# Last scaling of three of eight output tiles split between ScalarE and GpSimd, with the stores in another order

## The chip, the cores and the metric

The kernel runs on one core of a Trainium2 chip. The metric is the device time of one execution in microseconds. One core has five engines that run side by side, each with its own queue of instructions, and they meet at semaphores: TensorE (PE in the profile), VectorE (DVE), ScalarE (ACT), GpSimd (POOL) and SyncE (SP), the last of which issues only transfers here. The kernel is written by hand: the order of the instructions in each queue is the order of the code.

## The reference

One transformer layer on 1024 tokens of width 1024: four token mixers (top-k sparse attention, an mLSTM, banded attention, differential attention), a gated sum of them, then a mixture of 32 experts of which each token takes two, and a last RMS norm. The change concerns only what stands after the experts, which in the reference is this:

```python
def rmsnorm(x, g, eps=1e-6):
    xf = x.astype(jnp.float32)
    y = xf * lax.rsqrt(jnp.mean(xf * xf, axis=-1, keepdims=True) + eps)
    return (y * g.astype(jnp.float32)).astype(x.dtype)

# hier_moe: the experts' rows, weighted, are added up by token
out = jnp.zeros((t, d), h.dtype).at[row_tok].add((ys * row_w[:, None]).astype(h.dtype))
# hybrid_layer
return x + hier_moe(h2, ...)
# reference
return rmsnorm(x, final_norm_g)
```

## The kernel before, in words

The program runs through `project`, `attend`, `mix`, `route`, `experts` and `combine`. `combine` is the last 43 us of 1849. It works on eight tiles of 128 tokens (partitions) by 1024 columns, each 512 KB in fp32. The residual stream `s.x2[t]` lies in SBUF throughout, and the experts' rows lie in HBM in `ys`.

- **GpSimd** issues two indirect gathers for each tile (L2531): `ya[t]` and `yb[t]`, the two expert rows of each token, 16 transfers in all, in the order of the tiles.
- **VectorE** waits for both (`y_in[t]`), adds them into `x2[t]` with their gates (L2562, L2564: two `scalar_tensor_tensor`, each with two tensors in SBUF as inputs, and each followed by a wait for its own completion, the helper `link`), tells ScalarE (`summed`, L2566), and then finishes the tile before, `finish(t - 1)`: a reciprocal of 128 numbers (L2555), and the last scaling `ya = x2 * rms * fg` (L2556), a third `scalar_tensor_tensor` with two tensors in SBUF. `fg` holds the weights of the last norm on all partitions. After the last tile it does `finish(7)`.
- **ScalarE** squares and sums each row (L2542) and takes the root (L2545), into `rms`.
- **SyncE** waits for the scaled tiles and stores them in the order of the tiles (L2521), and then waits until all eight stores have landed (L2523).

Each engine's queue is in order. So a wait in SyncE's queue holds back all stores behind it, and the scaling of tile t - 1 stands between the sums of tile t and of tile t + 1 on VectorE.

Of other places the prediction uses rows from GpSimd's and VectorE's work earlier in the program: copies of a bias table (L390 to L392), a product of two tensors in SBUF (L400), the norm's scaling at the program's start (L597), and in the experts' loop a copy of 96 indices (L2247) beside VectorE's subtractions (L2452).

Of the kernel before, what the change touches and what calls it, by code (L numbers as in the profile page):

```python
# [20 lines left out]
ALU = mybir.AluOpType  # L21
ACT = mybir.ActivationFunctionType
# [5 lines left out]
NT = SEQ // P  # L28
# [44 lines left out]
def chained(eng, chain):  # L73


    sem, count = chain

    def link(ins):
        count[0] += 1
        ins.then_inc(sem, 1)  # L80
        eng.wait_ge(sem, count[0])
    return link


def build(nc, a):

    ctx = ExitStack()
    with ctx:
# [140 lines left out]
        s.sem = late_sem  # L229
        experts(nc, a, s)  # L230
        combine(nc, a, s)
    return nc

# [2268 lines left out]
def combine(nc, a, s):  # L2502

    sb, sem = s.sb, s.sem
    ya = [sb(f"ya{i}", [P, DM], 96 + 4 * i) for i in range(NT)]
    yb = [sb(f"yb{i}", [P, DM], 128 + 4 * i) for i in range(NT)]
    fg = sb("fg", [P, DM], 160)
    junk = sb("junk6", [P, DM], 164)
    ssq, rms, eps = sb("ssq6", [P, NT], 200), sb("rms6", [P, NT], 200.0625), sb("eps6", [P, 1], 200.125)
    fg_in, eps_set = sem("fg_in"), sem("eps_set")  # L2510
    squared = s.squared
    y_in = [sem(f"y_in{t}") for t in range(NT)]
    stored = s.x_in
    summed, rooted, final = sem("summed6"), sem("rooted6"), sem("final")
    with nc.Block() as block:
        @block.sync
        def _(sp):
            sp.dma_start(fg[:, :], a["g_final"].partition_broadcast(P)).then_inc(fg_in, 16)
            for t in range(NT):
                sp.wait_ge(final, t + 1)  # L2520
                sp.dma_start(a["out"][t * P:(t + 1) * P, :], ya[t][:, :]).then_inc(stored[t], 16)  # L2521
            for t in range(NT):
                sp.wait_ge(stored[t], 48)  # L2523

        @block.gpsimd
        def _(pool):
            pool.memset(eps[:, :], EPS).then_inc(eps_set, 1)  # L2527
            for t in range(NT):
                for k, dst in enumerate((ya, yb)):
                    col = k * NT + t  # L2530
                    pool.indirect_dma_start(dst[t][:, :], None, s.ys,  # L2531
                                            bass.IndirectOffsetOnAxis(ap=s.row_of[:, col:col + 1].bitcast(U32), axis=0)
                                            ).then_inc(y_in[t], 16)

        @block.scalar
        def _(act):
            act.wait_ge(eps_set, 1)
            for t in range(NT):
                act.wait_ge(summed, t + 1)
                if t:  # L2540
                    act.wait_ge(rooted, t)
                nc.scalar.activation(junk[:, :], s.x2[t][:, :], ACT.Square,  # L2542
                                     accum_out=ssq[:, t:t + 1]).then_inc(squared, 1)
                act.wait_ge(squared, NT + t + 1)
                nc.scalar.activation(rms[:, t:t + 1], ssq[:, t:t + 1], ACT.Sqrt, bias=eps[:, 0:1],  # L2545
                                     scale=1.0 / DM).then_inc(rooted, 1)

        @block.vector
        def _(dve):
            link = chained(dve, s.dve_chain)  # L2550
            dve.wait_ge(fg_in, 16)

            def finish(t):
                dve.wait_ge(rooted, t + 1)
                link(nc.vector.reciprocal(rms[:, t:t + 1], rms[:, t:t + 1]))  # L2555
                nc.vector.scalar_tensor_tensor(out=ya[t][:, :], in0=s.x2[t][:, :], scalar=rms[:, t:t + 1], in1=fg[:, :],  # L2556
                                               op0=ALU.mult, op1=ALU.mult).then_inc(final, 1)

            for t in range(NT):
                x2 = s.x2[t][:, :]  # L2560
                dve.wait_ge(y_in[t], 32)
                link(nc.vector.scalar_tensor_tensor(out=x2, in0=ya[t][:, :], scalar=s.gates[:, 0, t:t + 1], in1=x2,  # L2562
                                                    op0=ALU.mult, op1=ALU.add))
                link(nc.vector.scalar_tensor_tensor(out=x2, in0=yb[t][:, :], scalar=s.gates[:, 1, t:t + 1], in1=x2,  # L2564
                                                    op0=ALU.mult, op1=ALU.add))
                nc.vector.engine_nop().then_inc(summed, 1)  # L2566
                if t:
                    finish(t - 1)
            finish(NT - 1)
# [56 lines left out]
```

## Time and profile before

| | us |
|---|---|
| median of 3 runs | 1848.51 |
| lowest and highest | 1845.42, 1849.59 |
| the profiled execution, its own time | 1850.85 |
| span of its records | 1849.1 |
| `combine`, from its first gather to the end of the span | 42.8 |
| VectorE busy from 1806 to 1849.1 | 31.6 |
| ScalarE busy there | 12.8 |
| GpSimd busy there | 16.7 |

The span goes from the first to the last record of the profiled execution; 1.75 us of its own time lie outside the span. Over the whole program TensorE is busy 94% of the span, but in `combine` it has no work at all. Times in the rows are microseconds from the span's start.

### The profile page before, as it was taken

The page shows a single profiled execution, that of the slowest core. Times are in us where ns is not written, and L with a number is a line of the kernel's source. Part 1 is how long each engine was busy: PE and PEld are TensorE (multiplying, and loading weights), DVE is VectorE, ACT ScalarE, POOL GpSimd, SP SyncE. Part 2 cuts the span into 40 slices and gives each one's busy share as a digit, 9 for nine tenths or more (in the row PEclk, how much of TensorE's full clock was granted, in tenths as well). Part 3 has the DMA queues.
Part 4 walks back from the last instruction along what each step waited for, and adds up shares of the span by engine and source line. Part 5 has one row for each costly group of instructions (what it writes and reads, how often), then busy time and mean ns, then how long its engine had stood idle before and what let it go on. Part 6 is the DMA issues. An engine that isn't in the chain of part 4 may idle for free. (4 is left out here: it accounts for less than half of the span.)

```text
span 1849.1 us, 24075 instructions
## 1 busy us (share of the span) xinstructions
PE 1737.8 (94%) x8726; PEld 1318.3 (71%) x8726; DVE 1456.1 (79%) x2108; ACT 941.6 (51%) x1207; POOL 151.2 (8%) x129
## 2 busy tenths in 40 slices
PE   7999999999999999999999989959999999999990
PEld 7768877777777777777777767747777777777760
DVE  5587869989788878766528975679999999999976
ACT  6533121133344445554656520137788778777862
POOL 1100000000000000000000000002121221221103
PEclk9999999999999999999999989969999999999995
DMA  5202222112343421412316830199999999999947
GB/s 199 69 6 87 74 86 69 58 57 75 128 157 114 128 63 58 148 52 77 107 35 221 309 127 35 47 374 343 395 403 396 396 405 395 401 399 394 404 180 288
DMA packets 75920, 358.76 MB, mean 194 GB/s; under 512 B 8636, under 2 KB 11228, under 8 KB 49340
## 3 DMA queue, kind: packets, MB, share of 16 engines
q1 hardware_dynamic: 66364, 324.08, 46.9%
q0 software_dynamic: 5888, 20.97, 3.5%
q10 hardware_dynamic: 3584, 12.58, 1.7%
q8 instruction: 52, 0.85, 0.2%
q14 instruction: 32, 0.26, 0.0%
HBM read 301.63 MB, written 55.98 MB: 193 GB/s over the span
## 5 line engine op out<-in xcount | busy, mean ns | idle before, releaser
L2444 DVE TENSOR_TENSOR wa_lo<-wa,w_hi 128x2048 fp32r<-128x2048 f32 x127 | 287.6, 2286 | 15.5 <-ACT w_hi L2349 14.1
L2349 ACT ACTIVATE w_hi<-wa 128x2048 fp32r<-128x2048 f32 x127 | 242.8, 1915 | 63.0 <-PE psum L2293 36.4
L1470 PE MATMUL psum<-h_hi,w_hi 128*128 128x512 f32 x512 | 213.3, 417 | 4.0 <-DVE w_lo L153 2.1
L1470 PE MATMUL psum<-h_hi,w_lo 128*128 128x512 f32 x512 | 205.9, 402 | 0.0
L1470 PE MATMUL psum<-h_lo,w_hi 128*128 128x512 f32 x512 | 203.5, 397 | 0.0
L167 DVE MAX8 top<-sel 128x8 f32<-128x384 f32 (+5 forms) x192 | 171.3, 892 | 4.8
L165 DVE MATCH_REPLACE8 sel<-top,sel 128x384 f32<-128x384 f32 (+5 forms) x192 | 168.1, 876 | 0.0
L2273 PE MATMUL psum<-w_hi,xT_hi 128*96 128x512 f32 x512 | 164.9, 403 | 1.9 <-DVE xT_lo L2460 1.9
L2452 DVE TENSOR_TENSOR wb_lo<-wd,w_hi 128x2048 fp32r<-128x2048 f32 x62 | 139.4, 2289 | 33.4 <-ACT w_hi L2359 33.4
L2273 PE MATMUL psum<-wa_lo,xT_hi 128*96 128x512 f32 x512 | 160.7, 395 | 0.0
L2273 PE MATMUL psum<-w_hi,xT_lo 128*96 128x512 f32 x512 | 160.7, 395 | 0.0
L1470 PEld LDWEIGHTS psum<-h_hi,w_hi 128*128 128x128 f32 x512 | 97.0, 190 | 46.5 <-issue 18.9
L1197 ACT ACTIVATE pt<-psum 128x512 f32<-128x512 f32 (+3 forms) x144 | 61.2, 471 | 119.3 <-PE psum L1490 119.1
L2359 ACT ACTIVATE w_hi<-wd 128x2048 fp32r<-128x2048 f32 x62 | 118.7, 1915 | 3.8 <-PE psum L2273 2.4
L922 PE MATMUL psum<-h_hi,w_hi 128*128 128x512 f32 x288 | 117.6, 408 | 0.0
L1470 PEld LDWEIGHTS psum<-h_hi,w_lo 128*128 128x128 f32 x512 | 96.9, 189 | 25.3 <-issue 5.1
L922 PE MATMUL psum<-h_hi,w_lo 128*128 128x512 f32 x288 | 112.7, 391 | 0.0
L922 PE MATMUL psum<-h_lo,w_hi 128*128 128x512 f32 x288 | 112.4, 390 | 0.0
L1470 PEld LDWEIGHTS psum<-h_lo,w_hi 128*128 128x128 f32 x512 | 97.2, 190 | 19.6 <-issue 2.7
L2273 PEld LDWEIGHTS psum<-wa_lo,xT_hi 128*96 128x96 f32 x512 | 83.4, 163 | 36.0
L2273 PEld LDWEIGHTS psum<-w_hi,xT_lo 128*96 128x96 f32 x512 | 83.3, 163 | 35.8 <-issue 0.2
L2273 PEld LDWEIGHTS psum<-w_hi,xT_hi 128*96 128x96 f32 x512 | 78.6, 164 | 29.5 <-DVE xT_lo L2460 2.2
(388 smaller groups left out, 3396.5 us busy)
## 6 DMA issues: line engine op xcount, KB each, us to landing
wa<-expert_up SPq DMA_DIRECT2D x128, 1024.0 KB, 11.2
wd<-expert_down SPq DMA_DIRECT2D x64, 1024.0 KB, 11.3
w<-w_gate SPq DMA_DIRECT2D x32, 512.0 KB, 4.2
gate_pre<-gate_out SPq DMA_DIRECT2D x64, 256.0 KB, 2.6
gate<-gate_pre SPq DMA_DIRECT2D x32, 512.0 KB, 6.1
ys<-yo ACTq DMA_DIRECT2D x32, 384.0 KB, 6.9
w<-w_T SPq DMA_DIRECT2D x18, 512.0 KB, 3.8
ys<-zeros SPq DMA_DIRECT2D x7, 1152.0 KB, 5.9
```

Of the source, the lines that this page charges most:

```text
L165: link(nc.vector.match_replace(sc, top8[:, :], sc, TAKEN))
L167: link(nc.vector.max(top8[:, :], sc))
L922: ins = nc.tensor.matmul(psum[:, bank + h, :], w[:, k, :], x[:, k, h * 512:(h + 1) * 512], start=(k == 0 and r == 0), stop=(k == KC - 1 an ...
L1197: nc.scalar.activation(dst, src, ACT.Copy).then_inc(pt_copied, 1)
L1470: ins = nc.tensor.matmul(psum[:, 7, :], w[:, k, :], x[:, k, half * 512:(half + 1) * 512], start=(n == 0), stop=(n == BURST - 1))
L2273: ins = nc.tensor.matmul(psum[0:CAP, UP + m, :], x[:, k, :], w[:, c, m, :], start=(k == 0 and x is xT_hi[j] and w is not wa_lo[j][q]), sto ...
L2349: nc.scalar.activation(hi_a(j, q).rearrange("p c m n -> p (c m n)"), wa[j][q][:, :, :, :].rearrange("p c m n -> p (c m n)"), ACT.Copy).the ...
L2359: nc.scalar.activation(dst.rearrange("p f n -> p (f n)"), wb[j][q][:, :, :].rearrange("p f n -> p (f n)"), ACT.Copy).then_inc(b_high, 1)
L2444: nc.vector.tensor_tensor(wa_lo[j][q][:, :, :, :].rearrange("p c m n -> p (c m n)"), wa[j][q][:, :, :, :].rearrange("p c m n -> p (c m n)" ...
L2452: nc.vector.tensor_tensor(wb_lo[j][q][:, :, :].rearrange("p f n -> p (f n)"), wb[j][q][:, :, :].rearrange("p f n -> p (f n)"), high.rearra ...
```

## The change

Tiles 1, 3 and 5 (the second, fourth and sixth) are no longer scaled by VectorE. VectorE still takes the reciprocal for them. ScalarE then multiplies `x2[t]` by the row factor into `ya[t]`, behind its root of tile t + 1, and GpSimd multiplies `ya[t]` by `fg` in place, behind all 16 gathers. SyncE stores the tiles in the order 0, 2, 1, 4, 3, 6, 5, 7, and waits for GpSimd's semaphore before tiles 1, 3 and 5. Nothing else in the program changes, and there are no further table loads on ScalarE.

```diff
+    ON_POOL = (1, 3, 5)
+    own = [t for t in range(NT) if t not in ON_POOL]
@@ sync
-            for t in range(NT):
-                sp.wait_ge(final, t + 1)
+            for t in (0, 2, 1, 4, 3, 6, 5, 7):
+                if t in ON_POOL:
+                    sp.wait_ge(final_pool, ON_POOL.index(t) + 1)
+                else:
+                    sp.wait_ge(final, own.index(t) + 1)
                 sp.dma_start(a["out"][t * P:(t + 1) * P, :], ya[t][:, :]).then_inc(stored[t], 16)
@@ gpsimd, behind the gathers
+            pool.wait_ge(fg_in, 16)
+            for n, t in enumerate(ON_POOL):
+                pool.wait_ge(scaled, n + 1)
+                pool.tensor_tensor(ya[t][:, :], ya[t][:, :], fg[:, :], ALU.mult).then_inc(final_pool, 1)
@@ scalar, behind the root of tile t
+                if t - 1 in ON_POOL:
+                    act.wait_ge(inverted, ON_POOL.index(t - 1) + 1)
+                    nc.scalar.activation(ya[t - 1][:, :], s.x2[t - 1][:, :], ACT.Copy,
+                                         scale=rms[:, t - 1:t]).then_inc(scaled, 1)
@@ vector, finish(t)
                 dve.wait_ge(rooted, t + 1)
+                if t in ON_POOL:
+                    nc.vector.reciprocal(rms[:, t:t + 1], rms[:, t:t + 1]).then_inc(inverted, 1)
+                    return
```

VectorE's queue from the sum of tile 6 to the end, of the kernel before. In the names `x_6` is `s.x2[6]`, `ya_13441` is `ya[5]`, `ya_13442` is `ya[6]`, `ya_13443` is `ya[7]`, and ISA is the empty instruction that tells ScalarE of the sum:

```order
L2562 SCALAR_TENSOR_TENSOR x_6_9459<-ya_13442,gates,x_6_9459 128x1024
L2564 SCALAR_TENSOR_TENSOR x_6_9459<-yb_13450,gates,x_6_9459 128x1024
L2566 ISA
L2555 RECIPROCAL rms_13455<-rms_13455 128x1
L2556 SCALAR_TENSOR_TENSOR ya_13441<-x_5_9458,rms_13455,fg 128x1024
L2562 SCALAR_TENSOR_TENSOR x_7_9460<-ya_13443,gates,x_7_9460 128x1024
L2564 SCALAR_TENSOR_TENSOR x_7_9460<-yb_13451,gates,x_7_9460 128x1024
L2566 ISA
L2555 RECIPROCAL rms_13455<-rms_13455 128x1
L2556 SCALAR_TENSOR_TENSOR ya_13442<-x_6_9459,rms_13455,fg 128x1024
L2555 RECIPROCAL rms_13455<-rms_13455 128x1
L2556 SCALAR_TENSOR_TENSOR ya_13443<-x_7_9460,rms_13455,fg 128x1024
```

The same stretch of VectorE's queue in the changed kernel:

```order
L2579 SCALAR_TENSOR_TENSOR x_6_9459<-ya_13442,gates,x_6_9459 128x1024
L2581 SCALAR_TENSOR_TENSOR x_6_9459<-yb_13450,gates,x_6_9459 128x1024
L2583 ISA
L2570 RECIPROCAL rms_13455<-rms_13455 128x1
L2579 SCALAR_TENSOR_TENSOR x_7_9460<-ya_13443,gates,x_7_9460 128x1024
L2581 SCALAR_TENSOR_TENSOR x_7_9460<-yb_13451,gates,x_7_9460 128x1024
L2583 ISA
L2572 RECIPROCAL rms_13455<-rms_13455 128x1
L2573 SCALAR_TENSOR_TENSOR ya_13442<-x_6_9459,rms_13455,fg 128x1024
L2572 RECIPROCAL rms_13455<-rms_13455 128x1
L2573 SCALAR_TENSOR_TENSOR ya_13443<-x_7_9460,rms_13455,fg 128x1024
```

The scaling of tile 5 between the two sums is gone, its reciprocal stays; the same holds for tiles 1 and 3 further up.

The end of GpSimd's queue in the changed kernel, where before it ended with the two gathers (`ya_13437` and `ya_13439` are `ya[1]` and `ya[3]`):

```order
L2537 DMA ya_13442<-ys,row_of 128x1024
L2537 DMA yb_13450<-ys,row_of 128x1024
L2537 DMA ya_13443<-ys,row_of 128x1024
L2537 DMA yb_13451<-ys,row_of 128x1024
L2543 TENSOR_TENSOR ya_13437<-ya_13437,fg 128x1024
L2543 TENSOR_TENSOR ya_13439<-ya_13439,fg 128x1024
L2543 TENSOR_TENSOR ya_13441<-ya_13441,fg 128x1024
```

Three products of two tensors in SBUF have come in behind the last gather.

## Rows read from the trace of the kernel before

**Rows 1.** Chain that ended last, in order of time, from 1838.91: start, length, what.

```profile
1838.91 0.15 DVE rms L2555
...
1839.09 1.28 DVE ya L2556
1840.37 1.21 DVE x L2562
...
1841.61 1.30 DVE x L2564
...
1842.98 1.16 ACT junk L2542 x2
...
1844.16 0.30 ACT rms L2545
...
1844.69 1.29 DVE ya L2556
```

**Rows 2.** Groups from 1805 to 1850: busy us, mean ns, idle before and releaser.

```profile
L2556 DVE SCALAR_TENSOR_TENSOR ya<-x,rms,fg 128x1024 f32<-128x1024 f32 x8 | 10.3, 1285 | 0.3
L2562 DVE SCALAR_TENSOR_TENSOR x<-ya,gates,x 128x1024 f32<-128x1024 f32 x8 | 10.3, 1282 | 19.6 <-DMA yb<-ys,row_of 19.6
...
L2542 ACT ACTIVATE junk<-x 128x1024 f32<-128x1024 f32 x8 | 8.5, 1057 | 30.1 <-DVEq L2566 30.1
...
L2545 ACT ACTIVATE rms<-ssq,eps 128x1 f32<-128x1 f32 x8 | 2.4, 294 | 0.2
L2542 ACT ACTIVATION_READ_ACCUMULATOR junk<-x 128x1 f32 x8 | 1.5, 186 | 0.0
...
L2555 DVE RECIPROCAL rms<-rms 128x1 f32<-128x1 f32 x8 | 1.3, 159 | 0.4
```

**Rows 3.** Issue of yb for tiles 3 and 7, then the landing of each after its issue.

```profile
1816.09 0.94 POOL L2531 DMA_INDIRECT yb<-ys,row_of  x1 [0.30 <-issue]
1826.58 0.97 POOL L2531 DMA_INDIRECT yb<-ys,row_of  x1 [0.30 <-issue]
```
```profile
yb<-ys,row_of POOLq DMA_INDIRECT x1, 6.2
```
```profile
yb<-ys,row_of POOLq DMA_INDIRECT x1, 9.5
```

**Rows 4.** Timeline, start and length, of VectorE and GpSimd work that overlaps or stands alone.

```profile
19.26 1.29 DVE L597 SCALAR_TENSOR_TENSOR xs<-xs,rstd,gain 128x1024 f32<-128x1024 f32 x1
19.37 2.92 POOL L390 COPY far<-rel 128x2044 f32<-128x2044 f32 x1 [16.53 <-DMA rel<-rel]
22.25 0.82 POOL L391 COPY far<-rel 128x768 f32<-128x768 f32 x1
23.01 0.41 POOL L392 COPY far<-rel 128x260 f32<-128x260 f32 x1
```
```profile
1228.96 0.18 POOL L2247 COPY idx<-tok_of 96x1 int32 x1 [13.40 <-PE psum L2153]
```
```profile
1272.20 4.49 DVE L2452 TENSOR_TENSOR wb_lo<-wd,w_hi 128x2048 fp32r<-128x2048 f32 x2 [0.98 <-ACT w_hi L2359]
1273.12 1.41 POOL L2247 COPY idx<-tok_of 96x1 int32 x1 [13.30 <-PE psum L2153]
```

**Rows 5.** GpSimd's product of two SBUF tensors, line L400: ns min/median/max, first and last start.

```profile
L400 POOL TENSOR_TENSOR oB<-oB,gainB x8: 725/732/737, 52.4 to 57.2; 128x256 f32<-128x256 f32 x8
```

**Rows 6.** VectorE's first sum, line L2562: ns min/median/max.

```profile
L2562 DVE SCALAR_TENSOR_TENSOR x<-ya,gates,x x8: 1278/1279/1301, 1812.4 to 1840.3; 128x1024 f32<-128x1024 f32 x8
```

**Rows 7.** The last two stores: issue; landing; then windows of the transfer (last columns: clock, DMA share, GB/s).

```profile
1844.44 0.33 SPq L2521 DMA_DIRECT2D out<-ya  x1
```
```profile
1846.00 0.33 SPq L2521 DMA_DIRECT2D out<-ya  x1
```
```profile
out<-ya SPq DMA_DIRECT2D x1, 512.0 KB, 2.6
```
```profile
1846.50:1847.00 0.50, 0.00 (x0) 0.00 (x0) 0.00 (x0) 0.00 (x0) 0.00 (x0) 0.50 0.42 164
1847.00:1847.50 0.50, 0.00 (x0) 0.00 (x0) 0.00 (x0) 0.00 (x0) 0.00 (x0) 0.50 1.04 426
1847.50:1848.00 0.50, 0.00 (x0) 0.00 (x0) 0.00 (x0) 0.00 (x0) 0.00 (x0) 0.50 1.00 410
1848.00:1848.50 0.50, 0.00 (x0) 0.00 (x0) 0.00 (x0) 0.00 (x0) 0.00 (x0) 0.50 0.20 74
```

More of the change, by code:

```diff
@@ L2514, in combine @@
     summed, rooted, final = sem("summed6"), sem("rooted6"), sem("final")
+    inverted, scaled, final_pool = sem("inverted6"), sem("scaled6"), sem("final_pool")
+    ON_POOL = (1, 3, 5)
+    own = [t for t in range(NT) if t not in ON_POOL]
     with nc.Block() as block:
```

## Prediction

> **What bounds the kernel now.** The change lies wholly in the last 43 us, so I read first the chain of work that ended last, in order of time, and only its end. In [rows 1] the reader is to see that VectorE carries it almost alone: reciprocal, scaling of the tile before, two sums, again and again; a round is 4.04 us, six rounds in a row from tile 1 to tile 7. Only at the very end does ScalarE come in (1.16 + 0.30 us, square and root of tile 7), then the last reciprocal and scaling, which ends at 1844.69 + 1.29 = 1845.98. From there to the end of the span are 3.1 us of store. The groups of the same stretch [rows 2] say the same: the 24 large operations of VectorE take 1.28 us each and have no idle time before them but 19.6 us for gathers, all of it before tiles 0 and 1. ScalarE waits 30.1 us for VectorE. So an instruction taken from VectorE between tile 1 and tile 7 shortens the path, if nothing else holds it. Next I ask what would be late after that: gathers, ScalarE, GpSimd, the stores.
>
> **Part 1, three scalings leave VectorE: -3.7 us.** Each is 1.285 us [rows 2]. In [rows 1] the time from the end of a reciprocal (1839.06) to the start of the following sum, which overlaps the end of the scaling by 0.08, is about 1.3; without the scaling the sum starts about 0.05 after or at the reciprocal's end. That is 1.24 us a piece, and 3 x 1.24 = 3.7.
>
> **Part 2, the gathers stay hidden.** A faster VectorE asks for them earlier. The sum of tile 3 would start at about 1822.9; its last gather is issued at 1816.09 and lands 6.2 later, at 1822.3 [rows 3]. The tightest later one is tile 7: 1826.58 + 9.5 = 1836.1 [rows 3], against a sum that would start at 1840.37 - 3.7 = 1836.6 if VectorE gained everything. Cost 0; if that cover were gone by a store's more traffic it would be some tenths, but the changed order puts a store less among the gathers.
>
> **Part 3, ScalarE: off the path, 0.** After the root of tile 2, 4, 6 it has one more pass over 1024 columns. The nearest row is its square, 1.06 us [rows 2]. A round of ScalarE is 1.06 + 0.19 + 0.29 = 1.54 and becomes 2.7 in three rounds, where VectorE gives it at least the 2.6 of two sums. What is queued behind the new wait for the reciprocal is the square of the next tile; the reciprocal is ready by then, 0.2 us after the sum, while ScalarE is busy 1.6 with square and root. Before the last tile the copy of tile 5 ends 2.75 us after tile 6's sum, just before tile 7's sum ends at 2.83, so the last square isn't late.
>
> **Part 4, GpSimd's three products and what they do to VectorE: this decides.** Their own price first. The trace has a product of two SBUF tensors on GpSimd at 256 columns: 0.73 us each, eight started from 52.4 to 57.2, so one each 0.70 [rows 5]. What of it is fixed, the copies tell: 0.41 us for 260 columns, 0.82 for 768 [rows 4], so about 0.2 fixed in a recorded duration and 0.14 in the distance of starts (22.25 to 23.01 is 0.76 for 768). So at 1024 columns 4 x 0.56 + 0.14 = 2.4 us; the bound above is 4 x 0.73 = 2.9, the one below the rate of a copy, 1.0. I take 2.4, since it is the same operation and only its length differs.
>
> Now the two engines beside each other. In [rows 4] GpSimd's copy of 2044 columns is recorded from 19.37, while VectorE works on two SBUF inputs from 19.26 to 20.55, and takes 2.92. By the copies beside it it needs 0.14 + 2044 x 0.81 ns = 1.8; 20.55 + 1.74 is just where it ends, 22.29. It stood still for the whole of VectorE's instruction and then ran at its own speed. In the experts' loop a copy of 96 indices takes 0.18 us alone and 1.41 beside a VectorE pair of 2 x 2.25 us, and ends at 1274.53, the moment in which VectorE's first operation ends, though the second is queued right behind it (28 such copies have a median of 1.47). So GpSimd waits out the VectorE instruction that runs, and gets in at its end, ahead of or beside the next one. What happens to a VectorE instruction with two SBUF inputs that finds GpSimd in a long operation, this trace doesn't show: the long ones of GpSimd met no such VectorE work. The nearest row is one sum that lasted 1.301 instead of 1.278 [rows 6], beside a gather's issue that reads only its indices. So VectorE's loss per product lies between 0 and the whole 2.4 us. I take the whole, since in the direction that the trace shows the waiting side got no share until the other had ended.
>
> The Trainium skill, "SBUF — State Buffer", section "Who interferes with whom", says the same of both directions: a VectorE instruction with two SBUF inputs and a GpSimd instruction that reads SBUF take turns on a shared read interface, and whichever starts first keeps it for its whole length. The first direction this trace bears out (1.41 us in place of 0.18), the second no row here shows. The "GPSIMD Engine Reference", section 3.1, gives 4497 ns for such a product of 2048 columns; half, 2.25 us, would make the sum below 0.4 us smaller, an estimate from that page.
>
> Place by place: the first product stands behind the 16th gather, whose issue ends at about 1827.8. VectorE is then in the first sum of tile 4, to 1828.2. The product gets in there and holds back the second sum: 2.35 us. The second product (tile 3) is ready 2.75 us after the sum of tile 4, just when the sum of tile 5 ends; VectorE still has its reciprocal and semaphores (0.2), then the scaling of tile 4 waits: 2.4 - 0.2 = 2.2. The third (tile 5) comes in the same way at the end of tile 7's sum and holds back the scaling of tile 6: 2.2. Should VectorE come first at one of these points, the product only moves behind that instruction and holds the next; the sum stays. Together +6.75, less 0.15 for each start of a product in which it doesn't read yet, +6.3.
>
> **Part 5, the stores: +0.9 us.** The last store takes 0.8 us from issue to its first data and 1.25 us of data (512 KB at 410 to 426 GB/s, see the windows), landing in 2.6 [rows 7]. In the forecast case tiles 6 and 5 are both ready when the scaling of tile 6 ends, E. SyncE issues 6 at E and 5 at E + 0.33 (its issue takes 0.33), and tile 7 is scaled at E + 1.57, as 1844.44 to 1846.00 [rows 7]. Three transfers of 1.25 follow each other from E + 0.8: data ends at E + 4.55, against E + 1.57 + 0.8 + 1.25 = E + 3.6 for tile 7 alone. If the third product comes behind tile 6's scaling, stores 6 and 5 are apart and this term is 0.
>
> **Sum.** -3.7 + 6.3 + 0.9 = +3.5 us. On the profiled execution: 1850.85 + 3.5 = 1854.35, its span 1849.1 to 1852.6. That execution lies 2.3 above the median of the runs, so for the median: 1848.5 + 3.5 = 1852.0. With the product at 2.9 it is 1.5 more, 1853.5; without the term of the stores 1851.1; with both small (hold 2.1) 1850.5.
>
> **Rivals.**
>
> *VectorE isn't held (chance 0.14).* If a product that runs leaves VectorE's instructions their full speed, the 3.7 are gained in full, and the last product ends before tile 7's scaling: the copy of tile 5 is done 0.1 before tile 7's sum ends, + 2.4, against + 3.1 for VectorE's end. 1848.5 - 3.7 = 1844.8, faster. For it speaks only that no row shows VectorE held; against it, that the other direction is a full stop.
>
> *Sharing, or GpSimd comes last (0.16).* The two take turns in pieces, so that VectorE loses about half of each product: -3.7 + 3 x 1.2 = -0.1. Or VectorE always goes first when it has work, so that the third product waits until VectorE's last instruction has ended, at 1845.98 - 3.7 = 1842.3. It ends at 1844.7, and SyncE's queue has tile 7 behind tile 5: data of both ends at 1844.7 + 0.8 + 2.5 = 1848.0, where before it ended at 1848.1. That too is 0: 1848.4, no change. For it: a price between the ends; against it, the index copy that got in between two VectorE instructions.
>
> *The hold is longer than I make it (part of the first case, slower).* If a product at 1024 columns takes 2.9, by four times the 256 column row, VectorE loses 3 x 2.7 and the sum is +5. It decides from a hold of 2.2 us each on: above it the change passes 0.2% with the stores' term.
>
> The Trainium skill, "Perfetto Trace Analysis", section "Optimizing Scalar/DVE Operations", warns that work handed from VectorE to GpSimd may not help, since they share an SBUF port; the sum above is what that would mean here.
>
> **How the numbers follow.** The forecast case has 0.70: VectorE stands still for each product. Within it the time lies between 1850.5 and 1853.5 by the bounds, with a run's own scatter of some 2 us (1845.42 to 1849.59 before). The bound of 0.2%, 3.7 us, about what a measurement of this kernel can tell from no change, cuts through it at 1852.2: 0.39 above, 0.31 within. From the first rival (1844.8, just at the lower bound) 0.10 is faster and 0.04 within; from the second 0.13 within, 0.02 faster, 0.01 slower. So faster 0.12, same 0.48, slower 0.40. The time is that of the likeliest case, 1852.0. The range leaves out most of the first rival and the upper end with scatter: 1845.5 to 1855.0; the forecast case's own range is 1849.5 to 1855.
>
> **What the changed profile would show.** VectorE's operations at L2579, L2581 or L2573 with a maximum of 3 to 3.6 us in place of 1.3, three of them, each with a GpSimd product before it: right. All 21 at 1.28 and VectorE's last one ending near 1842.3: the first rival. Products of 4 us and more: GpSimd waits instead. The copy on ScalarE near 1.06, no wait of VectorE for gathers from tile 2 on, and stores of tiles 6 and 5 issued 0.33 apart. A product of 1.5 or of 4 us alone, or gathers that land later, would make the forecast wrong.

## The result

| | us |
|---|---|
| before, median of 20 runs (lowest, highest) | 1850.08 (1845.42, 1852.94) |
| changed, median of 20 runs (lowest, highest) | 1853.61 (1850.57, 1856.74) |
| ratio, with 95% interval | 1.0019 (1.0012 to 1.0026) |
| profiled execution of the changed kernel, its own time and span | 1856.19, 1854.4 |

The changed kernel is slower by 0.19%, 3.5 us between the medians; the interval, 2.2 to 4.8 us, excludes zero and straddles the 0.2% line. That is the sum of the prediction in size (+3.5) and its likeliest case. The time itself, forecast as 1852.0, came out 1.6 higher, since the forecast stood on the 1848.51 of three runs of the kernel before, and twenty give 1850.08. What follows asks whether the terms are as right as their sum.

The two spans differ by 5.3, but 2.4 of it lies ahead of `combine` (its first gather is issued at 1808.72, before at 1806.31), where the change touches nothing. So the traces are compared from that issue on. "VectorE's end" below is the time from the issue of the first gather to the end of VectorE's last operation, the "tail" is the time from there to the end of the span, and the "stretch" their sum:

| | VectorE's end | tail | stretch |
|---|---|---|---|
| before | 39.67 | 3.12 | 42.79 |
| changed | 41.39 | 4.29 | 45.68 |

Each such number is from one execution. VectorE's scaling of tile 0, ahead of which no edit takes anything from its queue or adds to it, starts 12.25 to 13.13 us after the first gather's issue in the fourteen traces. So VectorE's end can differ by up to 0.9 us between two executions before a product or a scaling left out has played any part. The lengths of single operations and the tails don't have this scatter.

The chain that ended last, of the changed kernel, in order of time (start, length, what), against [rows 1]:

```profile
1829.50 1.21 DVE x L2579
1830.70 0.02 issue
1830.73 3.25 DVE x L2581
1833.98 0.03 issue
1834.01 0.01 DVEq L2583
1834.03 0.14 DVE rms L2570
1834.17 1.20 DVE x L2579
...
1836.91 3.17 DVE ya L2573
...
1845.53 3.18 DVE ya L2573
...
1848.82 1.29 DVE ya L2573
```

VectorE still carries the chain. Behind the reciprocal of tile 3 (1834.03) the next sum starts at once: the scaling is gone. But three operations take 3.2 us, though they have the 1024 columns of those that take 1.28 in [rows 2]. The timeline of VectorE and GpSimd shows beside what they stand:

```profile
1830.32 2.57 POOL L2543 TENSOR_TENSOR ya<-ya,fg 128x1024 f32<-128x1024 f32 x1
1830.73 3.24 DVE L2581 SCALAR_TENSOR_TENSOR x<-yb,gates,x 128x1024 f32<-128x1024 f32 x1
...
1836.66 2.34 POOL L2543 TENSOR_TENSOR ya<-ya,fg 128x1024 f32<-128x1024 f32 x1 [3.77 <-ACT ya L2559]
1836.72 0.16 DVE L2572 RECIPROCAL rms<-rms 128x1 f32<-128x1 f32 x1
...
1836.91 3.17 DVE L2573 SCALAR_TENSOR_TENSOR ya<-x,rms,fg 128x1024 f32<-128x1024 f32 x1
...
1840.00 1.27 DVE L2579 SCALAR_TENSOR_TENSOR x<-ya,gates,x 128x1024 f32<-128x1024 f32 x1
...
1845.28 2.35 POOL L2543 TENSOR_TENSOR ya<-ya,fg 128x1024 f32<-128x1024 f32 x1 [6.28 <-ACT ya L2559]
1845.34 0.16 DVE L2572 RECIPROCAL rms<-rms 128x1 f32<-128x1 f32 x1
...
1845.53 3.18 DVE L2573 SCALAR_TENSOR_TENSOR ya<-x,rms,fg 128x1024 f32<-128x1024 f32 x1
```

Each long operation starts beside a product of GpSimd. The second product ends at 1839.00, the scaling beside it at 1840.08, as if it did nothing until 0.2 us before the product's end and then took its own 1.28. The two don't share in pieces either: the second and third product keep 2.34 and 2.35, as long as where they hold nobody (2.35 and 2.36 in kernels below). Nor is it that both want the same tile: the sum at 1830.73 reads `yb`, the gates and `x2`, the product beside it `ya[1]` and `fg`. What each lost is its length less 1.285: 1.96, 1.89 and 1.89, together 5.74 us. The reciprocal at 1836.72, one column with one input, ran its 0.16 within the same product.

The tail grew by 1.2 us. The windows of the last transfers (last columns: clock, DMA share, GB/s), against those of [rows 7], where the last store has the transfers to itself from 1846.50 on:

```profile
1850.00:1850.50 0.50, 0.00 (x0) 0.00 (x0) 0.10 (x1) 0.00 (x0) 0.00 (x0) 0.50 1.02 401
1850.50:1851.00 0.50, 0.00 (x0) 0.00 (x0) 0.00 (x0) 0.00 (x0) 0.00 (x0) 0.50 0.99 402
...
1852.00:1852.50 0.50, 0.00 (x0) 0.00 (x0) 0.00 (x0) 0.00 (x0) 0.00 (x0) 0.50 1.11 442
1852.50:1853.00 0.50, 0.00 (x0) 0.00 (x0) 0.00 (x0) 0.00 (x0) 0.00 (x0) 0.50 0.99 410
```

The transfers begin at about 1849.5, during VectorE's last operation, and run without a pause to about 1853.4: the last store stands behind two others.

### The profile page after: what moved, and what is told of

The parts are those of the page before. It is cut to its first block and busy times, and to the rows that moved or that the text cites. A ratio compares the mean times of both kernels' runs of the same rounds, so it can differ in the third digit from the quotient of the medians.

```text
span 1854.4 us, 24079 instructions
## 1 busy us (share of the span) xinstructions
PE 1738.8 (94%) x8726; PEld 1318.0 (71%) x8726; DVE 1459.6 (79%) x2105; ACT 945.1 (51%) x1210; POOL 158.8 (9%) x132
```

## The experiments

The theory: while GpSimd's product reads SBUF, a VectorE operation with two inputs in SBUF stands still, and the tail is the order of the stores. The rivals: ScalarE's extra passes or the traffic slow VectorE; any work of GpSimd slows it; any VectorE operation is slowed. All numbers are from traces unless they are called a ratio or a median; ratios are timed against the kernel before on the same chip, with their 95% interval. A microsecond in them is 0.05%, so the traces tell more. The diffs are against the changed kernel if not said otherwise.

### The products left out

```diff
-                pool.tensor_tensor(ya[t][:, :], ya[t][:, :], fg[:, :], ALU.mult).then_inc(final_pool, 1)
+                pool.engine_nop().then_inc(final_pool, 1)
```

> The changed kernel without GpSimd's three products (tiles 1, 3 and 5 are stored without the weights of the last norm); the semaphores, ScalarE's passes and the order of the stores stay. Measure: from the issue of the first gather to the end of the span, 42.8 us before and 45.7 changed. Theory (VectorE stands still while a product runs): the three long VectorE operations are 1.28 again, VectorE's last one ends 3.9 us earlier than before, the stores of tiles 5 and 6 are no longer together, and the stretch is about 39.0, so 3.8 below the kernel before and 6.7 below the changed one; ratio to before 0.998. Rival (ScalarE's passes or the order of the stores cost the time): VectorE's operations stay long or the last store stays late, and the stretch is 42 to 45.

Measured: VectorE's end 36.62, tail 4.16, stretch 40.78; ratio 0.9989 (0.9980 to 0.9998). Groups of the stretch (busy us, mean ns, idle before and releaser):

```profile
L2581 DVE SCALAR_TENSOR_TENSOR x<-yb,gates,x 128x1024 f32<-128x1024 f32 x8 | 10.3, 1285 | 0.3
...
L2573 DVE SCALAR_TENSOR_TENSOR ya<-x,rms,fg 128x1024 f32<-128x1024 f32 x5 | 6.4, 1285 | 0.2
L2559 ACT ACTIVATE ya<-x,rms 128x1024 f32<-128x1024 f32 x3 | 3.4, 1132 | 0.0
```

All of VectorE's operations are at 1.28 again with ScalarE's passes in place, so the long ones belong to the products. Two of my numbers missed. VectorE's end came 3.05 earlier than before, not 3.9. The missing 0.85 is time for gathers: the sum of tile 1 starts 10.18 us after the first gather's issue, before 9.73, and a wait of 0.41 us for tile 7 is new:

```profile
1836.14 1.28 DVE L2579 SCALAR_TENSOR_TENSOR x<-ya,gates,x 128x1024 f32<-128x1024 f32 x1 [0.41 <-DMA yb<-ys,row_of]
```

And the tail is 4.16 without any product, so it isn't the products that lengthen it.

### GpSimd writes and doesn't read

```diff
-                pool.tensor_tensor(ya[t][:, :], ya[t][:, :], fg[:, :], ALU.mult).then_inc(final_pool, 1)
+                pool.memset(spare[n][:, :], 1.0).then_inc(final_pool, 1)     # 2560 columns, own tile each
```

> In place of each product GpSimd fills a spare tile of 2560 columns, which reads nothing and takes about 2.3 us, as long as the product (tiles 1, 3 and 5 lack the weights). Theory (it is the second input of VectorE that is held, by GpSimd's reading): no VectorE operation is longer than 1.3, the stretch is about 39.9, since the last fill still delays the stores of tiles 5 and 7 by up to 0.9. Rival (any long GpSimd operation on SBUF holds VectorE): three VectorE operations of 3.2 us and the stretch 45 to 45.7 as in the changed kernel.

Measured: VectorE's end 35.98, tail 4.20, stretch 40.18; ratio 0.9986 (0.9977 to 0.9995).

```profile
1839.28 2.23 POOL L2544 MEMSET spare<- 128x2560 f32 x1 [4.51 <-ACT ya L2560]
...
1839.57 1.28 DVE L2574 SCALAR_TENSOR_TENSOR ya<-x,rms,fg 128x1024 f32<-128x1024 f32 x1
```

A GpSimd operation of 2.23 us lies over a whole VectorE scaling, which takes 1.28. Writing alone holds nothing; it needs GpSimd to read. The stretch was 0.3 above the 39.9 expected, within the scatter.

### The products alone, on the kernel before

```diff
+            pool.wait_ge(fg_in, 16)
+            for n, t in enumerate((1, 3, 5)):
+                pool.wait_ge(rooted, t + 2)
+                pool.tensor_tensor(spare[n][:, :], fg[:, :], fg[:, :], ALU.mult)
```

> The kernel before with three GpSimd products of the same size added behind the gathers, into spare tiles, each released by the root of tiles 2, 4 and 6; VectorE keeps all its scalings and the stores their order. Theory: each product holds one VectorE sum by about 1.95 us, together 5.9: the stretch 42.8 + 5.9 = 48.7, ratio to before 1.003; no term of the stores, since the last three tiles are apart. Rival (the loss in the changed kernel comes from ScalarE's part or from the stores): the stretch stays near 42.8 to 43.5.

Measured: VectorE's end 45.53, tail 3.13, stretch 48.66, 5.87 above before as expected; ratio 1.0022 (1.0013 to 1.0031), a little less than that. The hit is partly luck. Timeline:

```profile
1826.24 3.60 DVE L2561 SCALAR_TENSOR_TENSOR ya<-x,rms,fg 128x1024 f32<-128x1024 f32 x1
1826.84 1.91 POOL L2538 TENSOR_TENSOR spare<-fg 128x1024 f32<-128x1024 f32 x1
...
1833.99 2.83 POOL L2538 TENSOR_TENSOR spare<-fg 128x1024 f32<-128x1024 f32 x1 [5.25 <-ACT rms L2550]
...
1835.11 2.80 DVE L2569 SCALAR_TENSOR_TENSOR x<-yb,gates,x 128x1024 f32<-128x1024 f32 x1
```

The holds are 2.32, 1.51 and 1.51, together 5.3; the other half microsecond lies ahead of them (the first scaling starts 13.1 after the first gather, before 12.6), where no product has run yet. The second and third product come 0.2 us after the start of a sum; the second waits it out to 1835.07 and ends at 1836.82, 1.75 us later. In the changed kernel the first product also waits out a sum, to 1830.69 (1829.41 + 1.28), and ends 2.20 us later, at 1832.89. So a product of `fg` by itself is the shorter one, and the hold is shorter with it. Both directions are in these rows: GpSimd waits for the running sum, and the next sum waits for GpSimd.

### Half a product

```diff
-                pool.tensor_tensor(ya[t][:, :], ya[t][:, :], fg[:, :], ALU.mult).then_inc(final_pool, 1)
+                pool.tensor_tensor(ya[t][:, 0:512], ya[t][:, 0:512], fg[:, 0:512], ALU.mult).then_inc(final_pool, 1)
```

> The changed kernel, GpSimd multiplies only the first 512 of the 1024 columns (the other half of tiles 1, 3 and 5 lacks the weights). Measured so far: 0.73 us at 256 columns and 2.35 at 1024, so 1.27 at 512, and a hold of 1.96, 1.89 and 1.89 us at 1024. Theory (the hold lasts as long as the product does): each hold gets shorter by the product's 1.08, to 0.8 to 0.9 us, the three long VectorE operations take 2.1 to 2.2, VectorE's end 38.1 after the first gather's issue and the stretch 42.3 with the tail of 4.2. Rival (a hold is a fixed price of switching): they stay at 3.2 us and the stretch at 45.7.

Measured: VectorE's end 38.20, tail 4.36, stretch 42.56; ratio 1.0002 (0.9991 to 1.0012).

```profile
1832.66 1.27 POOL L2543 TENSOR_TENSOR ya<-ya,fg 128x512 f32<-128x512 f32 x1 [3.76 <-ACT ya L2559]
...
1832.92 2.10 DVE L2573 SCALAR_TENSOR_TENSOR ya<-x,rms,fg 128x1024 f32<-128x1024 f32 x1
```

The three long operations take 2.17, 2.10 and 2.08, holds of 0.89, 0.82 and 0.80. The second and third product, shorter by 1.08, hold for 1.07 and 1.10 less: a hold is the product's recorded length less 0.46 at either length, and no fixed price. (The first product's record, 1.49 here and 2.57 in the changed kernel, begins with some 0.2 us of waiting for the sum before it, so its hold is its record less 0.6.)

### The weights in PSUM for VectorE

```diff
+            nc.scalar.activation(fg_psum, fg[:, :], ACT.Copy).then_inc(fg_up, 1)
@@ vector, finish(t)
-  ... in0=s.x2[t][:, :], scalar=rms[:, t:t + 1], in1=fg[:, :],
+  ... in0=s.x2[t][:, :], scalar=rms[:, t:t + 1], in1=fg_psum,
```

> The changed kernel, but VectorE takes the weights for its scaling from a copy in PSUM, so that its scaling has one input in SBUF only. Theory (only an operation with two SBUF inputs is held): the first product holds the second sum of tile 4 as before (3.2 us); the second and third no longer hold the scalings of tiles 4 and 6, which take about 1.3; the second product then holds the first sum of tile 6 for the rest, 2.3 - 1.5 = 0.9, and the third nothing. So 3.8 of held time become 0.9 and VectorE ends 2.9 earlier; the stretch is 43 to 43.5, with the collision of the last stores. Rival (GpSimd and VectorE slow each other whatever VectorE reads): scalings of 3.2 us remain, the stretch stays at 45.7.

Measured: VectorE's end 39.75, tail 4.16, stretch 43.91; ratio 1.0006 (0.9997 to 1.0015). The third product and the scaling beside it:

```profile
1840.13 2.36 POOL L2545 TENSOR_TENSOR ya<-ya,fg 128x1024 f32<-128x1024 f32 x1 [7.80 <-ACT ya L2563]
...
1840.40 1.28 DVE L2577 SCALAR_TENSOR_TENSOR ya<-x,rms,psum 128x1024 f32<-128x1024 f32 x1
```

This is the row to set against the 3.18 at 1845.53 of the changed kernel: the same operation at the same place beside the same product, with one of its inputs in PSUM, and nothing is lost. All five scalings take 1.28. VectorE's gain fell short of 2.9 (it was 1.6) and the stretch is 0.4 above what I allowed, since the first two products came at other places than I had worked out and met two sums, which still read twice from SBUF:

```profile
1826.96 3.18 DVE L2583 SCALAR_TENSOR_TENSOR x<-ya,gates,x 128x1024 f32<-128x1024 f32 x1
...
1830.18 3.24 DVE L2585 SCALAR_TENSOR_TENSOR x<-yb,gates,x 128x1024 f32<-128x1024 f32 x1
```

### The stores of tiles 5 and 6 exchanged

```diff
-            for t in (0, 2, 1, 4, 3, 6, 5, 7):
+            for t in (0, 2, 1, 4, 3, 5, 6, 7):
```

> The changed kernel with the stores of tiles 5 and 6 exchanged (0, 2, 1, 4, 3, 5, 6, 7), nothing else. From the first gather's issue the changed kernel has 41.4 us to VectorE's end and 4.3 from there to the end of the span; before had 39.7 and 3.1. Theory (the longer tail comes from the order: tile 5 is ready 1.1 us before tile 6 and waits behind it in SyncE's queue, so that three transfers of 1.25 us stand in a row): VectorE's end stays at 41.4, the tail falls to 3.1 to 3.4, the stretch from 45.7 to 44.7. Rival (the tail is longer since the last transfers are slower or later for another reason): tail 4.2.

Measured: VectorE's end 41.45, tail 3.22, stretch 44.67; ratio 1.0003 (0.9994 to 1.0012). One microsecond of the loss was the order alone: tile 5 is ready when its product ends (1847.63 in the changed kernel) and waits in SyncE's queue behind tile 6 (1848.71), so that three transfers of 1.25 us meet at the end.

### First sums in PSUM too

```diff
@@ on top of the weights in PSUM: the first sum goes to PSUM, the second reads it there
-  scalar_tensor_tensor(out=x2, in0=ya[t][:, :], scalar=s.gates[:, 0, t:t + 1], in1=x2,
+  scalar_tensor_tensor(out=part, in0=ya[t][:, :], scalar=s.gates[:, 0, t:t + 1], in1=x2,
-  scalar_tensor_tensor(out=x2, in0=yb[t][:, :], scalar=s.gates[:, 1, t:t + 1], in1=x2,
+  scalar_tensor_tensor(out=x2, in0=yb[t][:, :], scalar=s.gates[:, 1, t:t + 1], in1=part,
```

> As the kernel with the weights in PSUM, and VectorE also writes the first sum of each tile to PSUM, so that the second sum has one input in SBUF; only the first sum of each tile still has two. Theory: long VectorE operations are to be found at the first sum only (L number of the sum of ya), one or two of them, held together 1.5 to 2.8 us where the changed kernel has 5.7; second sums and scalings all 1.28 to 1.35. VectorE's end 37 to 38.5 after the first gather's issue, tail 4.2 (the order 6, 5, 7 stays), stretch 41.5 to 42.7. Rival (VectorE is slowed by reading or writing PSUM): operations of 1.4 and more, and the stretch above 43.

Measured: VectorE's end 39.34, tail 4.19, stretch 43.53; ratio 1.0001 (0.9992 to 1.0010).

```profile
1823.15 4.02 DVE L2584 SCALAR_TENSOR_TENSOR psum<-ya,gates,x 128x1024 f32<-128x1024 f32 x1
...
1823.72 2.35 POOL L2546 TENSOR_TENSOR ya<-ya,fg 128x1024 f32<-128x1024 f32 x1
...
1832.62 1.99 DVE L2584 SCALAR_TENSOR_TENSOR psum<-ya,gates,x 128x1024 f32<-128x1024 f32 x1
```

The place was right, only first sums are held, and PSUM costs nothing (second sums and scalings 1.281 us), so the rival's sign is absent, although its stretch, above 43, came. The size was not right: I had allowed 1.5 to 2.8 of holds and it is 3.4, since the first product holds for 2.7 and not 1.9. That sum started 0.57 us before the product's recorded start and yet stood still from about its own start on. The product follows directly on the last gather's issue there, and GpSimd seems to have begun to read before its record starts. The last section returns to this.

### x2 of tiles 5 and 6 in PSUM

```diff
+            for t in (5, 6):
+                nc.scalar.activation(x_psum(t), s.x2[t][:, :], ACT.Copy).then_inc(fg_up, 1)
@@ and their first sums read it there
+  in1=x_psum(t) if t in (5, 6) else x2
```

> As the one before, and ScalarE copies x2 of tiles 5 and 6 to PSUM at the start, so that their first sums have one input in SBUF too. Theory: no VectorE operation is held at all if the three products fall on tiles 5 to 7; the first product may still meet the first sum of tile 4 or 7. VectorE's end 36.5 to 37 after the first gather's issue as without products (36.6), where now the gathers' landing bounds it, tail 4.2: stretch 40.8 to 41.2, 1.8 below the kernel before (0.999). Rival (sharing is not only by SBUF inputs): some operations stay at 3.2 and the stretch above 42.

Measured: VectorE's end 38.66, tail 4.13, stretch 42.79, the same as before; ratio 1.0003 (0.9994 to 1.0013). One hold is left, the first sum of tile 4 with 4.02 again, a hold of 2.7, more than the 1.6 to 2 us by which the stretch missed. The second and third product hold nothing.

### The first product later

```diff
@@ on top of that: the first product also waits for the root of tile 4
+                if n == 0:
+                    pool.wait_ge(rooted, 5)
```

> As the kernel with x2 of tiles 5 and 6 in PSUM (stretch 42.8, one operation of 4.02 us), but GpSimd's first product also waits for the root of tile 4, so that it isn't directly behind the last gather and meets only VectorE work with one SBUF input. Theory (the 4.02 is the first sum of tile 4, which still has two SBUF inputs and is held by that product, from half a microsecond before its recorded start): no VectorE operation above 1.3, VectorE's end 38.7 - 2.7 = 36.0, up to 36.6 with waits for gathers, the stretch 40.2 to 40.9. Rival (the 4.02 is the price of something else in PSUM or of the gathers): it stays, the stretch stays at 42.8.

Measured: VectorE's end 35.56, tail 4.18, stretch 39.74; ratio 0.9988 (0.9977 to 0.9998). No VectorE operation is above 1.3 us, and the stretch is 0.5 below the range, within the scatter. A wait added to GpSimd's queue made the stretch 3 us shorter.

### Tiles 1, 2 and 3 instead, with and without PSUM

```diff
-    ON_POOL = (1, 3, 5)
+    ON_POOL = (1, 2, 3)
-            for t in (0, 2, 1, 4, 3, 6, 5, 7):
+            for t in range(NT):
```

On the changed kernel, all in SBUF:

> The changed kernel with tiles 1, 2 and 3 handed over and the stores in the order of the tiles, all inputs in SBUF as in the kernels before and changed. Theory (in the fastest kernel so far, stretch 39.9, it is the inputs in PSUM that avoid the holds, not the choice of tiles): three holds, together 5.5 to 6.5 us, against 3.9 taken from VectorE; its end 41.3 to 42.3, the tail 3.1, the stretch 44.4 to 45.4, ratio about 1.001. Rival (the choice of tiles does it): no or one hold, the stretch 40 to 41.5.

Measured: VectorE's end 41.81, tail 3.14, stretch 44.95; ratio 1.0011 (1.0002 to 1.0020). Three holds of 1.7, 2.0 and 1.8, together 5.4, so the choice of tiles doesn't avoid them. The three products, one behind the other, are stretched in their turn:

```profile
1826.48 9.26 POOL L2543 TENSOR_TENSOR ya<-ya,fg 128x1024 f32<-128x1024 f32 x3
...
1827.30 2.96 DVE L2579 SCALAR_TENSOR_TENSOR x<-ya,gates,x 128x1024 f32<-128x1024 f32 x1
1830.30 3.24 DVE L2581 SCALAR_TENSOR_TENSOR x<-yb,gates,x 128x1024 f32<-128x1024 f32 x1
...
1833.78 3.06 DVE L2573 SCALAR_TENSOR_TENSOR ya<-x,rms,fg 128x1024 f32<-128x1024 f32 x1
```

The single products start at 1826.48, 1829.14 and 1832.42 and take 2.69, 3.31 and 3.33: the engines take strict turns here, product, sum, product, sum, product, scaling.

On top of weights, first sums and x2 of tiles 5 and 6 in PSUM:

> As the one before, but tiles 1, 2 and 3 are the ones handed over and the stores go in the order of the tiles, so that the last tiles are scaled by VectorE. Theory: the products lie between the end of the gathers' issue (21.5 us after the first) and 30, VectorE's end is 36.5 to 37, the tail 3.1 to 3.3 as before: stretch 39.8, 3 us below the kernel before, ratio 0.998. Rival (the gathers or the stores in the middle become the bound): VectorE waits 1 us and more for tiles 5 to 7, and the stretch is 41 to 42.

Measured: VectorE's end 36.81, tail 3.08, stretch 39.89; ratio 0.9983 (0.9972 to 0.9994). The same kernel in another set of runs:

> The same kernel as e10_tiles_1_2_3 once more: weights, first sums and x2 of tiles 5 and 6 in PSUM, tiles 1, 2 and 3 handed over. Expected as there: stretch 39.9 against 42.8 before, ratio 0.998 to 0.9985. If the first run owed its 0.9983 to scatter, the ratio is 0.9995 or above.

Measured: VectorE's end 36.88, tail 3.09, stretch 39.97; ratio 0.9980 (0.9971 to 0.9989), median 1845.62. Its products and VectorE's operations beside them:

```profile
1826.02 6.99 POOL L2551 TENSOR_TENSOR ya<-ya,fg 128x1024 f32<-128x1024 f32 x3
...
1826.96 1.29 DVE L2591 SCALAR_TENSOR_TENSOR psum<-ya,gates,psum 128x1024 f32<-128x1024 f32 x1 [0.25 <-DMA yb<-ys,row_of]
1828.29 1.28 DVE L2594 SCALAR_TENSOR_TENSOR x<-yb,gates,psum 128x1024 f32<-128x1024 f32 x1
...
1829.80 1.28 DVE L2585 SCALAR_TENSOR_TENSOR ya<-x,rms,psum 128x1024 f32<-128x1024 f32 x1
```

Without holds the stretch is 2.9 and 2.8 us below the kernel before, and both ratios are below 1, so this kernel is faster than before by 0.2%, and than the changed kernel (1.0019) by about 0.4%. What is missing to the forecast 3.7 went to gathers: VectorE waits three times 0.25 to 0.34 us for them after tile 0 in this trace, for tiles 1, 4 and 5, and the sum of tile 1 starts 0.5 us later than before.

## Why the prediction was right

**Part 1, the scalings leave VectorE.** Forecast -3.7. From the start of a reciprocal to the start of the next sum it is 1.39 us with the scaling (1838.90 to 1840.29 in the timeline of the kernel before) and 0.08 without (1825.31 to 1825.39 in the changed kernel), 1.31 each, 3.9 in all. I had let the sum start at the reciprocal's end or after it; it starts 0.08 before it.

**Part 2, the gathers.** In the changed kernel VectorE waits for none after tile 1, as forecast. But the cover was as thin as it looked: in the kernel without products VectorE waits 0.41 us for tile 7, whose last gather lands 10.3 us after its issue there, against 9.5 before, 9.8 in the changed kernel and 8.8 in the one that only writes. Why it varies isn't shown. The first rival, too, was mis-sized. The kernel without products stands for it, and gained 2.0 us, not 3.7: 0.65 less on VectorE, and 1.04 of longer tail, which that rival put at nothing. It would have given some 1846.5 in place of 1844.8.

**Part 3, ScalarE.** Its new pass takes 1.13 us, not 1.06. A long round takes 2.52 (1825.36 to 1827.88); the prediction's 2.7 is more than its own terms add up to (1.54 + 1.06 = 2.6). It made nothing late: from tile 1 on the squares start 0.09 to 0.10 after their sums, as before.

**Part 4, the hold.** A product takes 2.35 (forecast 2.4). All three got in where the prediction put them: before the second sum of tile 4, and before the scalings of tiles 4 and 6. They held for 1.96, 1.89 and 1.89, where the forecast was 2.35, 2.2 and 2.2, less 0.15 each; 5.7 in place of 6.3. The difference is mostly at the end: in all twenty holds of these kernels the held operation ends 1.08 to 1.10 us after the product's recorded end, 0.2 less than its own 1.28. The step that no row of before showed, a VectorE operation that waits for GpSimd, is shown now by four experiments: it goes when the products are left out, it isn't there when GpSimd only writes, it shrinks with the product, and it goes when one of VectorE's inputs lies in PSUM. So what the Trainium skill says in "SBUF — State Buffer", section "Who interferes with whom", holds here in both directions and with its conditions, two SBUF inputs on VectorE and a GpSimd instruction that reads SBUF; the hold only ends 0.2 us before the product's record. The Trainium skill's figure in "GPSIMD Engine Reference", section 3.1, is for an addition of 2048 columns, not a product; 2.25 us, an estimate from half of it, is 0.1 below the measured 2.35.

**Part 5, the stores.** Forecast +0.9, measured 1.17. The mechanism was half right: three transfers meet, but I laid that to the products' coming late, and wrote that the term would vanish if a product came behind the scaling of tile 6. It comes with the order 6, 5, 7: the kernel without products keeps a tail of 4.16, and exchanging 5 and 6 takes it to 3.22.

**Sum.** -3.9 + 5.7 + 1.2 = +3.0, and the stretch grew by 2.9. The forecast was +3.5: the holds were 0.6 too long, the saving 0.2 too small and the stores' term 0.3 too small, and the errors partly cancel. That the medians say +3.5 as well is luck to the tenth, since their interval is 2.2 to 4.8. The lower bound of 1850.5 doesn't follow from the hold of 2.1 given for it: three holds of 2.1 are the 6.3 of the forecast case, which gives 1851.1 without the stores; 1850.5 takes holds of 1.9. Both rivals are excluded by the rows: VectorE is held, and the products neither share in pieces nor come last.

## What to carry to other kernels

Before work goes from VectorE to GpSimd, count the tensor inputs in SBUF of the VectorE operations that will run beside it: here each microsecond of a reading GpSimd operation beyond about the first half microsecond was lost to a two-input operation of VectorE, and 3 x 1.9 us lost outweighed 3 x 1.3 won. If PSUM is free, one input or an intermediate result there took the hold away at no cost in VectorE's time. And put a queue of stores in the order in which tiles are ready, above all the last three: one exchange was worth 1 us.

## What was not expected

- A product directly behind a gather's issue can hold VectorE from before its recorded start. In three kernels a two-input operation started 0.57 to 0.60 us before it and stood still from its own start (4.02 us twice, and the 3.60 of the products alone, a hold of 2.32 by a product recorded with 1.91). Operations that started 0.8 us or more before it, as in the changed kernel, ran their 1.28, and the product waited. Of the products with idle time ahead of them, two in the products alone came 0.20 us after the start of a sum and didn't hold it. So the early start goes with the place behind the issue. The issues before don't do it by themselves: no VectorE operation beside one took over 1.30 us in the kernel before. That GpSimd begins to read early there is the likely reading, not a shown one.
- The product of `fg` by itself into a spare tile is recorded with 1.91 us where it waited for nobody, that of two different tiles, in place, with 2.35. Which of the two differences matters stays open.
- VectorE's `scalar_tensor_tensor` of 1024 columns takes the same 1.28 us with two SBUF inputs, with one in PSUM, and with its output in PSUM (1.274 to 1.288 in the groups without a hold).
